# Gates fetched eight rows at a time in 1 KB pieces, with rings of four buffers for u and v

## The reference

```python
def peer_ffn(h, wq, subkeys, u, v):          # per block xc of 128 tokens
    q = (xc @ wq).reshape(C, PEER_HEADS, 2, PEER_DKEY // 2)
    ...                                      # two top-16 of 128 keys, then the best 16 of their sums, per head
    g = jax.nn.softmax(best_s, axis=-1)      # 8 heads x 16 experts for each token
    ue = jnp.take(u, idx, axis=0)            # 16384 experts of width 1024
    ve = jnp.take(v, idx, axis=0)
    act = jax.nn.gelu(jnp.einsum('cd,chkd->chk', xc, ue), approximate=False)
    return jnp.einsum('chk,chkd->cd', g * act, ve)
```

## Time and profile before

| | |
|---|---|
| median of 3 executions | 5084.98 us (5077.57 to 5086.27) |
| the profiled execution | 5085.8 us, span of its instructions 5083.9 us |
| busy TensorE / VectorE / ScalarE / GpSimd | 4344.4 / 3379.6 / 1212.5 / 1809.9 us |
| dense loop of layer 0 | about 1757 to 2950 us of the span |
| dense loop of layer 1 | about 4236 to 5040 us of the span |
| bytes moved by DMA | 1407.99 MB, 277 GB/s in the mean |

### The profile page before, as it was taken

One profiled execution on the slowest core, in us unless ns is written; L12 is line 12 of the kernel. 1 busy time (PEld: TensorE's weight loads), 2 busy tenths in 40 slices (PEclk: granted clock), 3 DMA queues, 4 the chain that ended last, 5 costly groups with the idle time before them and its releaser, 6 DMA issues. The chain is left out here.

```text
span 5083.9 us, 54536 instructions
## 1 busy us (share of the span) xinstructions
PE 4344.4 (85%) x18847; PEld 2963.1 (58%) x18847; DVE 3379.6 (66%) x7344; ACT 1212.5 (24%) x2191; POOL 1809.9 (36%) x1652
## 2 busy tenths in 40 slices
PE   7899976693888799999999977886747778999997
PEld 5677664382655566666676744552533435666665
DVE  2366665578888777776777745664687775666665
ACT  2222311110443311111111122331213332222222
POOL 0022111023766555554555500000237774444331
PEclk9899978797999899999999989997878989999999
DMA  6967775614999999999999927667338999999995
GB/s 232 321 185 215 209 207 161 212 50 145 356 370 347 362 365 358 357 355 345 372 355 362 353 86 223 174 190 220 120 109 326 362 341 352 357 357 356 359 356 194
DMA packets 514328, 1407.99 MB, mean 277 GB/s; under 512 B 45692, under 2 KB 128636, under 8 KB 509214
## 3 DMA queue, kind: packets, MB, share of 16 engines
q1 hardware_dynamic: 329758, 733.60, 44.3%
q0 software_dynamic: 184320, 671.17, 34.7%
HBM read 1226.33 MB, written 178.26 MB: 276 GB/s over the span
## 5 line engine op out<-in xcount | busy, mean ns | idle before, releaser
L1723 POOL DMA_INDIRECT expert_rows<-u_rows,peer_arena x640 | 883.1, 1380 | 1286.3 <-DVE expert_rows L2025 1059.7
L1768 PE MATMUL ps<-part_arena,peer_part_arena 128*128 128x384 f32 (+1 forms) x4096 | 1035.3, 335 | 33.4 <-DVE peer_part_arena L2068 31.5
L2025 DVE SCALAR_TENSOR_TENSOR expert_rows<-expert_rows,mixer_in 128x1024 f32<-128x1024 f32 x640 | 760.3, 1220 | 136.0 <-DMA expert_rows<-u_rows,peer_arena 133.9
L1730 POOL DMA_INDIRECT expert_rows<-in_peer_v,peer_arena x640 | 723.1, 1130 | 195.0 <-issue 181.9
L1740 PE MATMUL ps<-expert_rows,peer_arena 128*128 128x512 f32 x1024 | 531.3, 670 | 300.2 <-DVE peer_arena L2033 300.2
L1768 PEld LDWEIGHTS ps<-part_arena,peer_part_arena 128*128 128x128 f32 x4096 | 698.8, 190 | 96.3 <-issue 81.5
L1777 PE MATMUL ps<-best,peer_arena 128*128 128x512 f32 x1540 | 685.3, 592 | 0.0
L1768 PE MATMUL ps<-mixer_in_parts,peer_part_arena 128*128 128x384 f32 (+1 forms) x2048 | 633.0, 309 | 0.0
L1740 PEld LDWEIGHTS ps<-expert_rows,peer_arena 128*128 128x128 f32 x1024 | 209.7, 214 | 566.2 <-issue 291.2
L2052 DVE SCALAR_TENSOR_TENSOR peer_arena<-expert_rows,peer_arena 128x1024 f32<-128x1024 f32 x381 | 489.4, 1285 | 29.1 <-DVE peer_arena L2052 0.5
L1777 PEld LDWEIGHTS ps<-best,peer_arena 128*128 128x128 f32 x1540 | 285.0, 189 | 296.0 <-issue 296.0
(11 more groups left out here) (259 smaller groups left out, 6146.2 us busy)
## 6 DMA issues: line engine op xcount, KB each, us to landing
peer_arena<-in_peer_u SPq DMA_DIRECT2D x256, 512.0 KB, 8.3
best<-in_peer_v SPq DMA_DIRECT2D x154, 512.0 KB, 6.0
mixer_arena<-in_peer_u SPq DMA_DIRECT2D x272, 256.0 KB, 7.7
u_rows<-mixer_arena SPq DMA_DIRECT2D x136, 512.0 KB, 6.5
hidden<-in_peer_u SPq DMA_DIRECT2D x240, 256.0 KB, 6.2
u_rows<-hidden SPq DMA_DIRECT2D x120, 512.0 KB, 4.8
gates<-peer_arena SPq DMA_DIRECT2D x20, 2048.0 KB, 10.8
peer_arena<-in_peer_v SPq DMA_DIRECT2D x52, 512.0 KB, 6.0
```

What stands on the lines that cost most here:

```text
L1723: pool.indirect_dma_start(u_ring[:, k % U_SLOTS, :], None, u_table, bass.IndirectOffsetOnAxis(u_index[s][:, m:m + 1], 0)).then_inc(u_row_i ...
L1730: pool.indirect_dma_start(v_ring[:, k % V_SLOTS, :], None, v_table, bass.IndirectOffsetOnAxis(v_index[s][:, m:m + 1], 0)).then_inc(v_row_i ...
L1768: mm = pe.matmul(ps[:, 6, 0:dense_tok], left[j % len(left)][:, c, :], right[:, c, :], start=at == 0, stop=at == len(todo) - 1)
L2025: dve.scalar_tensor_tensor(out=rows, in0=rows, scalar=1.0, in1=B.x[:, :, rows_at + s * P:rows_at + s * P + P], op0=ALU.mult, op1=ALU.mult, ...
```

## The change

The gates of eight rows are fetched at once, where four were. A row's 32 tokens are 128 bytes, so that the contiguous piece in DRAM becomes 1024 bytes instead of 512, and the loads of gates are half as many, each with the same number of pieces and twice the bytes (1.5 MB in layer 0, 1 MB in layer 1). The two gate buffers double in size. The rings of u and of v have four buffers each instead of five, which gives the room; the v buffer that lay in `peer_arena` is the one that goes.

```diff
+GATE_ROWS = 8
...
-    BUFS = 5
+    BUFS = 4
...
-    v_space = [ar.take(D)] + [B.best[:, x * D:x * D + D] for x in range(3)] + [B.spare_arena[:, 3 * D:]]
+    v_space = [B.best[:, x * D:x * D + D] for x in range(3)] + [B.spare_arena[:, 3 * D:]]
     v = v_space[:BUFS]
-    g = [ar.take(QUAD * dense_tok).rearrange("p (n j t) -> p n j t", j=QUAD, t=TG) for _ in range(2)]
+    g = [ar.take(GATE_ROWS * dense_tok).rearrange("p (n j t) -> p n j t", j=GATE_ROWS, t=TG) for _ in range(2)]
...
-            if j % QUAD == 0:
-                if j >= 2 * QUAD:
-                    sp.wait_ge(wt_ok, j - QUAD)
-                sp.dma_start(g[j // QUAD % 2].rearrange("p n j t -> p n (j t)"),
-                             B.g_dram[0:nd * P // TG, :, j * TG:(j + QUAD) * TG].rearrange("n i k -> i n k")
-                             ).then_inc(g_in[j // QUAD % 2], 16)
+            if j % GATE_ROWS == 0:
+                if j >= 2 * GATE_ROWS:
+                    sp.wait_ge(wt_ok, j - GATE_ROWS)
+                sp.dma_start(g[j // GATE_ROWS % 2].rearrange("p n j t -> p n (j t)"),
+                             B.g_dram[0:nd * P // TG, :, j * TG:(j + GATE_ROWS) * TG].rearrange("n i k -> i n k")
+                             ).then_inc(g_in[j // GATE_ROWS % 2], 16)
...
-            if j % QUAD == 0:
-                dve.wait_ge(g_in[j // QUAD % 2], 16 * (j // QUAD // 2) + 16)
+            if j % GATE_ROWS == 0:
+                dve.wait_ge(g_in[j // GATE_ROWS % 2], 16 * (j // GATE_ROWS // 2) + 16)
```

More of the change, by code:

```diff
@@ L2122, in vector @@
             dve.tensor_tensor(wt[j % 2].rearrange("p (n t) -> p n t", t=TG), gelu[j % 2].rearrange("p (n t) -> p n t", t=TG),
-                              g[j // QUAD % 2][:, :, j % QUAD, :], ALU.mult).then_inc(wt_ok, 1)
+                              g[j // GATE_ROWS % 2][:, :, j % GATE_ROWS, :], ALU.mult).then_inc(wt_ok, 1)
             if j + 2 < KEYS:
```

## The result

| | before | changed |
|---|---|---|
| median | 5081.56 us (4 runs, 5077.57 to 5086.27) | 5123.95 us (4 runs, 5110.85 to 5130.84) |
| ratio | | 1.0069, 95% interval 1.0057 to 1.0082 |
| profiled execution | 5085.8 us | 5110.85 us, the quickest of the four |

The change makes the kernel slower by 0.7%; 5088 us was forecast. The medians lie 42 us apart, a quotient of 1.0083; the ratio, as it was estimated in the measurement, is 1.0069 or 35 us. The traced pair differs by 25.0 us only.

What follows compares the result with a forecast made beforehand. TensorE was taken to set the pace, with loads ahead of it. Only the loop starts cost, 1.8 + 1.2 = +3.0 us, the other parts nothing: from a median of 5084.98 to 5088 us, range 5080 to 5094, 8 in 10 5079 to 5100.

Steps and rivals of the forecast that it cites:

- What bounds the kernel: In the dense loops of `peer` TensorE sets the pace, with the loads ahead of it, except at each loop's start.
- Part 1: At each loop's start the larger first load of gates delays u[0]: 1.8 us in layer 0, 1.2 in layer 1, +3.0 us.
- the straight line: Price of a 1 KB packet of gates, interpolated between measured 512 B and 4 KB packets: 45.1 ns.
- Part 2: Fewer, larger gate packets in the loop save 0.7 us per eight rows of layer 0 on DMA engines; effect nothing.
- Part 3: Ring of u, issued one period later: u lands at 15.3 and 10.8 us, ScalarE waits 2.3 us, TensorE nothing.
- The limit of 12.6 us: Layer 1: latest landing of u after issue before TensorE waits; 1.8 us remained against the forecast 10.8 us.
- the slower rival: u of layer 1 lands too late, from 12.6 us on; +27 us at 14.4 us, 5115 us in all; chance 0.12.
- its limit of 23.2 us: Layer 0: latest landing of u after issue before TensorE waits; 7.9 us remained against the forecast 15.3 us.
- on ScalarE gelu(j-1), which a period covers: In the loops, gelu(j-1) queued on ScalarE behind a late u was claimed to be covered by one period.
- the sign that was named: TensorE waits inside the loop for the split or for wt would show the prediction wrong: u past 12.6 or 23.2 us.
- ScalarE's wait: In the loops, ScalarE waits for u behind each load of gates, about 30 times, some 2.3 us each.
- Part 4: Ring of v with four buffers: v[j] is needed over 20 us after its issue in both layers; effect nothing.

Runs made afterwards that it cites:

- experiment 2: Changed kernel with five buffers again for u and v, gates still eight rows at a time: 5090.92 us, 1.0008 of the kernel before.
- experiment 6: Changed kernel with the sparse work of j+1 ahead of the split of u[j+2] on VectorE, its gelus ahead of the rounding on ScalarE: 5089.90 us, 1.001.
- experiment 9: Changed kernel with four buffers for u and five for v: 5096.95 us, 1.0015 of the kernel before.
- experiment 10: Kernel before with the sparse work put ahead of the split, the edit of experiment 6: 5085.95 us, 0.9992 of the unedited kernel.
- its copy: Changed kernel run once more, unaltered, in a later session: 5114.08 us, 1.0063 of the kernel before.
- experiment 7: Changed kernel with each load of gates after the first issued one j earlier, ahead of u[8k-1] instead of u[8k]: 5094.28 us, 1.0017.
- experiment 8: Changed kernel with five buffers for u and four for v: 5120.05 us, 1.0068 of the kernel before.
- experiment 1: Kernel before with four buffers each for u and v, gates still four rows at a time: 5097.43 us, 1.0022.
- experiment 11: Changed kernel with the eight rows of gates fetched in two back-to-back DMAs of four rows, so pieces of 512 bytes: 5152.69 us, 1.012.

## Why the prediction was wrong

**What bounds the kernel**: right. With its loads in time TensorE keeps its pace whatever the loads look like (experiments 2, 6, 9, 10), and no change of the DMA traffic made the loops quicker.

**Part 1, the start, +3.0 us**: right in kind, low in size. Between the traced pair it is 3.0 + 2.9 = 5.9 us; in the seven traces with the big load ahead of u[0] (the changed kernel, its copy, experiments 2, 6, 7, 8 and 9) the wait for the first split lies between 14.9 and 20.2 us, in the three with the small one (before, 1 and 10) between 14.3 and 16.2 us; the means differ by 2.6 + 1.7 us, 4.4 in sum. The packet measured 49 ns; the straight line gave 45, and with 49 the sum is 2.2 + 1.5 us, 3.6 unrounded. The least transfer at line rate that the Trainium skill gives ("DMA: Bandwidth & Descriptors", Specifications), 512 bytes, would make it 52.6, twice 26.3. The trace does not agree: 314 GB/s with 512 bytes, 341 with 1 KB, 416 with 4 KB.

**Part 2, nothing in the loop**: right in that nothing is gained.

**Part 3, "the u lands at 13.5 + 1.8 = 15.3 and 9.6 + 1.2 = 10.8 us": this is the step that failed.** They landed after 18.2 and 13.5 us in the median, in layer 1 12.3 to 15.1 us. The limit of 12.6 us held there; the landing, the 9.6 + 1.2 of the sum, was mis-sized by 2.7 us. What was wrong is the sentence in the slower rival, "the order and phase of the loads within a period don't change". In layer 1 the gathers come every second j, and one buffer less moves gates and u from the half without gathers to the half with them. Experiment 7 moves the gates back, and u lands after 11.0 us, as good as the forecast. In layer 0, where gathers run in every j, the eight rows made u 4.2 us later (14.0 to 18.2), twice the 96 x 22.7 ns = 2.2 us of their packets. That gathers and gates taking turns on the same engines is the reason fits both, and is argued; the sizes are measured. Layer 0 could bear it, within its limit of 23.2 us, but for the first load of gates inside the loop: its u landed after 25.1 us, and from it came the wait of 3.2 us.

In the chain behind the landing the prediction named wt(j-1) for values(j-1). It is gelu(j-1) for scores(j), by way of the sparse products and their gelus; the two limits happen to lie together, and experiment 6 shows the chain by taking the products out of it. That is luck: "on ScalarE gelu(j-1), which a period covers" was wrong, and the sign that was named, a wait for the split or for wt, is not the one that came. ScalarE's wait, forecast at 2.3 us "behind each load of gates", came about 30 times as forecast, but took (94.1 - 19.4) / 16 = 4.7 us in the mean of layer 1 and (96.9 - 19.6) / 17 = 4.5 us in layer 0.

**Part 4, the ring of v, "nothing"**: wrong in effect. The loads of v are in time with four buffers, but u[j] waits in the queue for what v[j-1] waits for. The prediction used this time of issue in its numbers and still booked the loss to the ring of u. Experiments 8 and 9 turn that around: five buffers for u alone leave the loss (1.0068), five for v alone take most of it (1.0015).

**The rival** that the u of layer 1 comes too late is what happened: from 12.6 us on, about 15 times, with +27 us named for a landing of 14.4 us. Inside the loops of the traced pair the waits grew by 16.4 us and the loops by 24.2 us; the granted clock that fell behind the two longest waits and the 0.2 us or so that a wait costs beyond its row were in no sum. By the medians the change costs 42 us; the traced execution was the quickest of four, and what the others lost more was not seen. A chance of 0.12 was too small for a margin of 1.8 us against a landing that had been built up from packet prices alone.

## What to carry to other kernels

A margin of a prefetch ring is the landing time under load against the whole chain behind the landing, in the order of every engine's queue: go from the waiting instruction to whatever stands behind it, and ask which of it someone else needs first. Where two streams of DMAs have different periods, look at which of their phases meet, and do it again for the new depth of the ring. In an in-order queue the buffers of one stream set the issue of the other: two rings can't be judged one by one. And two small losses of the same margin can together be more than their sum (here 0.22% and 0.08% against 0.69%).

## What the runs showed of the hardware

- A packet of 512 bytes took 26.3 ns on a DMA engine, one of 1 KB 49 and one of 4 KB 158; the rates are 314, 341 and 416 GB/s.
- A load that is issued together with a burst of gathers lands later than the same load 6 us behind the start of the burst: 13.5 against 11.0 us for the u behind 1 MB of gates (the changed kernel and experiment 7, layer 1).
- The issue of a DMA can hold SyncE for long behind a load of many pieces, but not by their number alone. In layer 0 the issue of u behind the gates took, in the median, 1.5 us before (1536 pieces of 512 bytes), 2.9 us in the changed kernel (1536 of 1 KB) and 11.4 us in experiment 11 (3072 of 512 bytes). With the small load again it was 5 to 8.5 us in the slow pace of experiment 1, and in layer 1 it was 1.8 us before (1024 of 512 bytes) and 0.6 us in the changed kernel (1024 of 1 KB).
- Behind idle stretches of TensorE of 2.46 and 3.25 us the granted clock was at half, 0.50 and 0.51, for 3 us; behind one of 1.26 us it stayed at 1.00 (the changed kernel).
